# A float32 trunk layer with a two-level mixture of experts: rows scattered into one region per expert while projecting, contiguous expert steps, and the residual rows loaded a second time

## The chip, the cores and the metric

One core of one Trainium2 chip. The metric is the device time of one execution in microseconds (us), the median of several runs.

## The reference

One layer over 2080 rows of 1024 numbers (2048 of a prompt, 32 of a running stream), all in float32:

```
proj = x @ w_in ; gate_b, gate_c, val_a, val_b, gate_lru = split(proj)      # 512 columns each
u = gate_c * val_a ; y_a = gate_b * conv3(u)
xc = conv4(val_b) + bias ; y_b = rg_lru(xc) * gelu(gate_lru)                # 8 heads x 64
x = layer_norm(ALPHA * x + concat(y_a, y_b) @ w_out)
g = argmax(softmax(x @ w_router_group))                                      # 1 of 4 groups
top_v, top_i = top_k(expert logits of group g, 2)                            # 2 of its 4 experts
h = silu(x @ w1[e]) * (x @ w3[e]) * gate ; y = sum over the two experts of h @ w2[e]
x = layer_norm(ALPHA * x + y)
```

The outputs are the rows and the states (last inputs of both convolutions, last state of the recurrence), for prompt and stream. There are 16 experts with 256 hidden columns; each row goes to two of them.

## The kernel before

Every large product is made of three fp32r products: each operand is split into a high part (a copy on ACT, ScalarE) and a low part (a subtraction on DVE, VectorE), and PE (TensorE) adds high by high, high by low and low by high. The program is four blocks, one after the other; a block starts when all engines have left the one before. Inside a block the order on each engine is written out by hand, with semaphores between engines.

**Mixer and projection** (mixer and mix_project_phase, L72 to L882). The mixer goes over 4 channel groups (j), inside each over 5 chunks of 416 rows (c). A step on PE is five times 24 matmuls (L272) and six for the gates of the recurrence (L281). ACT and DVE turn the products into ya and yb, one buffer each, and SyncE stores them into y_scr (store_y, L209; stores L215, L216, L218). ACT's copy L336 of a step writes ya first and waits until the store of the step before has landed (L335); behind it on ACT stands xc_hi (L341), and on that hang DVE's xc_lo (L444) and PE's L281. Then 17 tiles of 128 rows: PE projects y (L742, 48 matmuls), DVE adds the residual row (L840), takes statistics (L845, L849), ACT normalises (L803), DVE multiplies (L863) and GpSimd adds (L701); the result x1 is stored by ACT into x1_scr (L806), and multiplied by ALPHA on ACT (L809) it is stored into acc_scr (L792). PE turns x1 (L753), ACT copies it (L788), PE makes the 20 router logits (L760), DVE copies them (L831). On PE the order of a tile t is project(t), route(t-2), turn(t-1).

**Routing** (route_phase, L934). With the logits of all 17 tiles, DVE picks groups and experts, PE counts rows (L1023, L1024), DVE works out a slot for each of the 4160 (row, expert) pairs, packed so that each expert starts on a multiple of 128, and builds one-hot tables (L1133, L1134) that PE multiplies into a table of row numbers and gates by slot (L1030). The first expert's weights are loaded and split meanwhile.

**Experts** (experts_phase, L1157). A step is 128 slots of one expert; the number of steps follows from the counts (42 here). GpSimd gathers the rows with an indirect DMA by row number (L1234); PE turns them (L1268), ACT and DVE split them (L1320, L1363), PE multiplies by w1 and w3 (L1296), ACT takes the silu (L1341), DVE multiplies by gate (L1383), PE turns that (L1303) and multiplies by w2 (L1280). The output half on ACT (L1326), half on DVE (L1369) goes to SBUF, and GpSimd adds it to acc_scr with an accumulating indirect DMA (L1246); one must have landed before the next is issued. In steps whose flag split is set the next expert's weights are split (L915, L920, L925, L929); SyncE loads weights (L1217, L1219).

**Last phase** (finish_phase, L1400). Per tile: load from acc_scr, statistics (L1453, L1456), ACT's square root and normalising pass, DVE's scale and shift (L1461, L1463), DVE's multiplication by the weight (L1459), GpSimd's addition of the bias (L1436), store.

## Time and profile before

| | us |
|---|---|
| median of 3 runs | 1322.22 |
| lowest, highest | 1317.29, 1328.05 |
| span of the profiled execution | 1314.2 |
| busy: PE, DVE, ACT, GpSimd | 1132.7, 710.5, 522.3, 298.0 |

The time of the profiled execution itself is not listed; its span, from the first to the last instruction, stands beside the three times. PEld is PE's loading of weights, which runs beside its matmuls; SPq, ACTq and POOLq are the queues of SyncE, ACT and GpSimd. A busy engine is not always the one that sets the end; the stages differ in that, and are looked at one by one.

### The profile page before, as it was taken

Reading aid. Unit: us, or ns where it says so; the run is one execution under the profiler, and the core shown is the slowest. Engines: PE = TensorE matmul, PEld = TensorE weight load, DVE = VectorE, ACT = ScalarE, POOL = GpSimd, SP = SyncE. Lnnn points to the kernel's source line nnn. Section 1 sums busy time; section 2 is a strip of 40 time slices with the busy share of each in tenths; the row PEclk is TensorE's granted clock in tenths of the full one; section 3 lists DMA queues with packets and bytes.
Section 4 is the critical chain, followed back from the end, with each engine's and each line's share of the span. In section 5 each row is a group of like instructions: output and inputs, shape, how many; then the busy total and the mean of one; then the engine's idle time right before and its main releaser. Section 6 shows DMA issues by size and latency. Waiting matters only on the chain. (4 is left out here: it accounts for less than half of the span.)

```text
span 1314.2 us, 19578 instructions
## 1 busy us (share of the span) xinstructions
PE 1132.7 (86%) x5748; PEld 1021.3 (78%) x5749; DVE 710.5 (54%) x1131; ACT 522.3 (40%) x678; POOL 298.0 (23%) x254
## 2 busy tenths in 40 slices
PE   6999999999999999999999269999999899996000
PEld 6999999999999998888887157877787778885000
DVE  5676544644555564434334755555646445531698
ACT  4554533634445453333333204444445434421222
POOL 1000000000000021121211242345535443432244
PEclk9999999999999999999999559999999999999555
DMA  5422100200120155544432535787888877764822
GB/s 181 137 85 74 56 19 19 97 19 19 35 88 13 52 166 190 173 144 160 144 128 100 205 112 179 212 279 200 267 224 233 257 194 207 206 125 62 324 112 100
DMA packets 64423, 183.95 MB, mean 140 GB/s; under 512 B 7456, under 2 KB 34096, under 8 KB 60176
## 3 DMA queue, kind: packets, MB, share of 16 engines
q1 hardware_dynamic: 42464, 104.28, 22.4%
q0 software_dynamic: 17040, 61.57, 19.1%
q10 hardware_dynamic: 4896, 17.83, 3.3%
q8 instruction: 10, 0.16, 0.1%
q14 instruction: 13, 0.11, 0.0%
HBM read 125.70 MB, written 57.96 MB: 140 GB/s over the span
## 5 line engine op out<-in xcount | busy, mean ns | idle before, releaser
L1296 PE MATMUL ps_h<-w_hi,xt_hi 128*128 x336 | 136.5, 406 | 0.0
L1296 PE MATMUL ps_h<-w_hi,xt_lo 128*128 x336 | 132.8, 395 | 0.0
L1296 PE MATMUL ps_h<-w_lo,xt_hi 128*128 x336 | 132.8, 395 | 0.0
L272 PE MATMUL ps_vb_c<-x_hi,w_hi 128*128 (+1 forms) x320 | 114.0, 356 | 10.7 <-DVE x_lo L424 10.7
L272 PE MATMUL ps_vb_c<-x_lo,w_hi 128*128 (+1 forms) x320 | 113.2, 354 | 0.0
L272 PE MATMUL ps_vb_c<-x_hi,w_lo 128*128 (+1 forms) x320 | 113.1, 353 | 0.0
L272 PE MATMUL ps_va_b<-x_hi,w_hi 128*128 (+1 forms) x320 | 112.3, 351 | 0.0
L272 PE MATMUL ps_va_b<-x_hi,w_lo 128*128 (+1 forms) x320 | 112.1, 350 | 0.0
L272 PE MATMUL ps_va_b<-x_lo,w_hi 128*128 (+1 forms) x320 | 111.9, 350 | 0.0
L1246 POOL DMA_INDIRECT acc_scr<-out_sb,id_s x42 | 76.2, 1813 | 35.4 <-POOL id_s L1242 27.9
L193 POOL DMA_DIRECT2D w_raw<-in_w_in x15 | 8.0, 531 | 328.8 <-DVE w_lo L410 320.4
L701 POOL TENSOR_TENSOR w_lo_p<-w_hi_p,w_lo_p 128x1024 f32<-128x1024 f32 x16 | 38.3, 2393 | 179.7 <-DVE w_hi_p L863 179.7
L920 DVE TENSOR_TENSOR w_lo<-w_raw,w_hi 128x2048 f32 (+1 forms) x31 | 72.4, 2335 | 11.7 <-ACT w_hi L915 11.7
L1296 PEld LDWEIGHTS ps_h<-w_hi,xt_lo 128*128 128x128 f32 x336 | 63.9, 190 | 13.8
L1296 PEld LDWEIGHTS ps_h<-w_hi,xt_hi 128*128 128x128 f32 x336 | 64.5, 192 | 12.4
L1296 PEld LDWEIGHTS ps_h<-w_lo,xt_hi 128*128 128x128 f32 x336 | 64.4, 192 | 12.5
L1268 PE MATMUL ps_x<-consts_sb,xg 128*128 128x128 f32 x336 | 47.2, 286 | 28.9 <-DMA xg<-x_scr,id_g 21.8
L272 PEld LDWEIGHTS ps_vb_c<-x_hi,w_hi 128*128 128x128 f32 x320 | 60.8, 190 | 11.6 <-issue 8.2
L1363 DVE TENSOR_TENSOR xt_lo<-ps_x,xt_hi 128x1024 fp32r<-128x1024 f32 x42 | 51.3, 1221 | 32.8 <-ACT xt_hi L1320 32.8
L1234 POOL DMA_INDIRECT xg<-x_scr,id_g x43 | 57.9, 1347 | 33.7 <-POOL id_g L1231 30.3
L1326 ACT ACTIVATE out_sb<-ps_o 128x512 f32<-128x512 f32 x42 | 25.1, 599 | 100.8 <-PE ps_o L1280 100.8
L1268 PEld LDWEIGHTS ps_x<-consts_sb,xg 128*128 128x128 f32 x336 | 38.7, 146 | 34.0 <-issue 27.1
(246 smaller groups left out, 2722.3 us busy)
## 6 DMA issues: line engine op xcount, KB each, us to landing
w_raw<-in_w SPq DMA_DIRECT2D x16, 2048.0 KB, 8.6
w_raw<-in_w SPq DMA_DIRECT2D x16, 1024.0 KB, 9.2
w_raw<-in_w_in POOLq DMA_DIRECT2D x19, 512.0 KB, 3.7
w_hi_p<-in_x_rows SPq DMA_DIRECT2D x17, 512.0 KB, 3.8
x_scr<-w_lo_p ACTq DMA_DIRECT2D x17, 512.0 KB, 2.6
acc_scr<-w_lo_p ACTq DMA_DIRECT2D x17, 512.0 KB, 2.6
v<-acc_scr SPq DMA_DIRECT2D x17, 512.0 KB, 10.5
x_raw<-in_x_t SPq DMA_DIRECT2D x20, 416.0 KB, 3.5
```

The source lines that it names most:

```text
L193: pool.dma_start(w_raw[:, i % 2], w_in[bass.ds(j * MT + i, 1)].rearrange("o p k n -> p (o k) n")).then_inc(s_wraw[i % 2], 16)
L272: mm = pe.matmul(ps[i][:, 0:CHUNK], w[:, i, k], x[:, k, bass.ds(c * CHUNK, CHUNK)], start=(k == 0 and n == 0), stop=(k == KT - 1 and n == 2))
L701: pool.tensor_tensor(x1[par], s_sb[par], ln_b, ALU.add).then_inc(s_x1, 1)
L920: eng.tensor_tensor(self.half(self.w13_lo, at, i), self.raw_half(i), self.half(self.w13_hi, at, i).bitcast(F32), ALU.subtract).then_inc(se ...
L1234: pool.indirect_dma_start(xg[:, par], None, x1_scr, bass.IndirectOffsetOnAxis(id_g[:, par:par + 1], 0)).then_inc(s_xg[par], 16)
L1246: pool.indirect_dma_start(acc_scr, bass.IndirectOffsetOnAxis(id_s[:, par:par + 1], 0), out[:, par], None, compute_op=ALU.add).then_inc(s_a ...
L1268: mm = pe.transpose(ps_x[:, k], xg[:, par, k * P:(k + 1) * P], consts[:, C_ID:C_ID + P])
L1296: mm = pe.matmul(ps_h[par][:], x[:, par, k], w[:, bass.ds(at, 1), k].rearrange("p o n -> p (o n)"), start=(k == 0 and n == 0), stop=(k == ...
L1326: act.activation(out[:, par, 0:512], ps_o[0][:], ACT.Copy).then_inc(s_oa, 1)
L1363: dve.tensor_tensor(xt_lo[:, par], ps_x[:], xt_hi[:, par].bitcast(F32), ALU.subtract).then_inc(s_xlo, 1)
```

## The change

It touches every block but leaves the products as they are.

- **Zero fills.** After channel group 0, DVE zeroes a strip of 256 columns, and SyncE issues 47 DMAs between the stores of group 0 and those of group 1: per expert, 128 rows of xs_scr and 128 entries of g_scr, then the output blocks of steps 33 to 47 of o_scr.
- **Projection.** Tiles go through a ring of eight buffers in SBUF, where they are loaded, summed and normalised in place by DVE alone (two passes, mean and weight, then 1/std and bias). The copies to x1_scr and acc_scr, ACT's two passes and GpSimd's addition are gone. PE's order is project(t) up to k = 5, turn(t-1), count matmuls, the rest of project(t), route(t-1).
- **Routing while projecting** (Router). For groups of two tiles (one of them has one) DVE assigns experts (assign) and works out places (places); each expert has a fixed region of 2080 rows in xs_scr, and a row's place is the count so far. GpSimd scatters each tile's rows twice and its gates twice with indirect DMAs (scatter). The last two groups are scattered in the experts' block, which follows at once. There, plan_steps makes the list of steps (expert, first row, split flag), the last step of an expert beginning so that it ends with its last row; slots() makes the table of output rows by token.
- **Experts.** SyncE loads 128 contiguous rows of xs_scr for PE, 128 gates, and the same 128 rows once more into another buffer. DVE evicts both halves of the output while it adds ALPHA/2 times those rows, and SyncE stores the block plainly into o_scr. Weights are loaded from GpSimd's queue. ACT evicts nothing.
- **Last phase.** GpSimd gathers the two output rows of each token; DVE adds them, takes statistics and makes both normalising passes; ACT has the square root alone.

The core of the diff:

```diff
+CAP = TOK
+ZC = 256
+XS = 4
+FEWEST = -(-TOPK * TOK // P)
+NRING = 8
+GROUPED = [(t, 2) for t in range(0, NT - 3, 2)] + [(NT - 3, 1), (NT - 2, 2)]
...
+        sp.wait_ge(s_zero, 1)
+        for e in range(NE):
+            sp.dma_start(xs_scr[e * CAP:e * CAP + P, :].rearrange("p (a d) -> p a d", d=ZC),
+                         zero.unsqueeze(1).broadcast_to((P, D // ZC, ZC))).then_inc(s_zo, 16)
+            sp.dma_start(g_scr[e * CAP:e * CAP + P, :], zero[:, 0:1]).then_inc(s_zo, 16)
+
+        for n in range(FEWEST, STEPS):
+            sp.dma_start(o_scr[n * P:n * P + P, :].rearrange("p (a d) -> p a d", d=ZC),
+                         zero.unsqueeze(1).broadcast_to((P, D // ZC, ZC))).then_inc(s_zo, 16)
         with sp.Fori(1, GROUPS - 1) as j:
...
+        dve.memset(zero, 0.0).then_inc(s_zero, 1)
...
+    def counts(self, pe, n, bank, before, ones):
+        m = GROUPED[n][1]
+        pe.wait_ge(self.s_asg, n + 1)
...
+        pe.matmul(bank[:, 0:m * NE], before, rhs, start=True, stop=True)
+        pe.matmul(bank[:, 2 * NE:(2 + m) * NE], ones, rhs, start=True, stop=True).then_inc(self.s_cnt, 1)
...
+    def scatter(self, pool, n):
+        t0, m = GROUPED[n]
+        pool.wait_ge(self.s_sl, n + 1)
+        todo = [(t, TAIL if t == NT - 1 else P, c) for t in range(t0, t0 + m) for c in range(TOPK)]
+        for t, rows, c in todo:
+            pool.indirect_dma_start(self.xs_scr, bass.IndirectOffsetOnAxis(self.sli[0:rows, t, c:c + 1], 0),
+                                    self.ring[t % NRING][0:rows], None).then_inc(self.s_sc[n % 4], 16)
+        pool.wait_ge(self.s_wts, n + 1)
+        for t, rows, c in todo:
+            pool.indirect_dma_start(self.g_scr, bass.IndirectOffsetOnAxis(self.sli[0:rows, t, c:c + 1], 0),
+                                    self.wts[0:rows, t, c:c + 1], None).then_inc(self.s_gs, 16)
...
+            early, late = list(range(KT - 2)), list(range(KT - 2, KT))
+            for t in range(NT):
+                project(t, early)
+                if t >= 1:
+                    turn(t - 1)
+                for n in ends_at(t - 2):
+                    if n == 0:
+                        pe.wait_ge(mx.s_gel, STEPS_MIX)
+                    rt.counts(pe, n, ps_c, before, ones)
+                project(t, late)
+                if t >= 1:
+                    route(t - 1)
+            turn(NT - 1)
+            route(NT - 1)
...
+                dve.scalar_tensor_tensor(out=v, in0=v, scalar=mv[:, par, 0:1], in1=ln_g,
+                                         op0=ALU.subtract, op1=ALU.mult).then_inc(s_xn, 1)
...
+                dve.scalar_tensor_tensor(out=v, in0=v, scalar=rstd[:, par:par + 1], in1=ln_b,
+                                         op0=ALU.mult, op1=ALU.add).then_inc(s_x1, 1)
+                for n in ends_at(t - 2):
+                    rt.places(dve, n, ps_c)
+                if t >= 1:
+                    logits_out(t - 1)
+                for n in ends_at(t - 1):
+                    dve.wait_ge(s_lo, t + 1)
+                    rt.assign(dve, n)
...
+            def load(s, par, h):
+                row = sp.value_load(plan[0:1, 1, bass.ds(s, 1)], min_val=0, max_val=NE * CAP - P)
+                read, there, free = (count(sp, v) for v in (s - 1, h * 32, s - (XS - 1)))
+                if not early(s, 2):
+                    sp.wait_ge(s_tx, read)
+                    sp.wait_ge(s_g[par], there)
+                sp.dma_start(xg[:, par], xs_scr[bass.ds(row, P), :]).then_inc(s_xg[par], 16)
+                if not early(s, XS):
+                    sp.wait_ge(s_ev, free)
+                sp.dma_start(gate[:, slot(par, h)], g_scr[bass.ds(row, P), :]).then_inc(s_g[par], 16)
+                sp.dma_start(flat(xr[:, slot(par, h)]), xs_scr[bass.ds(row, P), :]).then_inc(s_g[par], 16)
+
+            def store(s, par):
+                sp.wait_ge(s_ev, s + 1)
+                sp.dma_start(o_scr[bass.ds(s * P, P), :], out[:, par]).then_inc(s_st[par], 16)
+
+            def step(s, par, h, left):
+                if not early(s, 1):
+                    store(s - 1, 1 - par)
+                if left == 2:
+                    load(s + 3, 1 - par, h + 1 + par)
+
+            sp.dma_start(consts[:], consts_in).then_inc(s_con, 16)
+            sp.wait_ge(s_plan, 1)
+            for n in range(LAST - 3, LAST + 1):
+                sp.wait_ge(rt.s_sc[n % 4], rt.landed(n))
+            sp.wait_ge(rt.s_gs, 16 * TOPK * NT)
...
+            pool.dma_start(ew.w13_raw[:], w13[0]).then_inc(ew.s_r13, 16)
+            pool.dma_start(ew.w2_raw[:], w2[0]).then_inc(ew.s_r2, 16)
+            for n in (LAST - 1, LAST):
+                rt.scatter(pool, n)
...
-                act.activation(out[:, par, 0:512], ps_o[0][:], ACT.Copy).then_inc(s_oa, 1)
...
+            def evict(s, par, h):
+                dve.wait_ge(s_o, s + 1)
+                if not early(s, 2):
+                    dve.wait_ge(s_st[par], h * 16)
+                for f in range(2):
+                    c = slice(f * 512, f * 512 + 512)
+
+                    ins = dve.scalar_tensor_tensor(out=out[:, par, c], in0=flat(xr[:, slot(par, h), c]), scalar=ALPHA / 2,
+                                                   in1=ps_o[f][:], op0=ALU.mult, op1=ALU.add)
+                ins.then_inc(s_ev, 1)
...
+            rt.assign(dve, LAST)
+            rt.places(dve, LAST, ps_c)
+            dve.wait_ge(s_con, 16)
+            plan_steps()
+            ew.lo13(dve, 0, first)
+            ew.lo2(dve, 0, first)
             x_lo(0, 0)
+            slots()
...
+                for c, to in enumerate((v, v1)):
+                    pool.indirect_dma_start(to[0:n, t], None, o_scr,
+                                            bass.IndirectOffsetOnAxis(sfin[0:n, c, t:t + 1], 0)).then_inc(s_in[t], 16)
```

## Rows read from the trace of the kernel before

**Rows 1.** Stage windows: us, each engine's busy us (instructions), PE clock, DMA share, GB/s.

```profile
489.00:715.00 226.00, 225.51 (x1167) 191.74 (x1165) 94.17 (x181) 76.90 (x87) 41.50 (x21) 1.00 0.45 154
...
1207.00:1225.00 18.00, 0.07 (x1) 0.00 (x0) 0.75 (x2) 1.88 (x2) 1.75 (x2) 0.56 0.44 97
1225.00:1314.20 89.20, 0.00 (x0) 0.00 (x0) 81.41 (x102) 26.09 (x34) 39.76 (x17) 0.50 0.46 186
...
795.08:1184.52 389.44, 369.90 (x1794) 306.47 (x1795) 204.40 (x200) 164.59 (x199) 167.38 (x156) 0.99 0.76 217
```

**Rows 2.** Timeline around channel group 1's first steps: start, us, engine, line, operation.

```profile
143.35 0.43 SPq L216 DMA_DIRECT2D y_scr<-yb  x1
...
152.32 0.34 SPq L218 DMA_DIRECT2D y_scr<-ya  x1
...
166.19 0.52 ACT L336 ACTIVATE ya<-ps_vb_c 128x416 f32<-128x416 f32 x1 [2.10 <-PE ps_vb_c L272]
...
179.42 0.35 PE L281 MATMUL ps_r_i<-xc_hi,l_hi 128*128 128x420 f32 x1
```

**Rows 3.** DMA rates, 512 B pieces (window 662.7:668.5), 4 KB pieces (window 1223:1240).

```profile
GB/s 424 29 0 0 395 28 56 56 254 311 339 367 395 367 254 343 251 265 219 343 343 353 360 346 346 339 346 314 191 39 11 0 0 0 0 0 0 0 0 0
...
DMA packets 1893, 6.91 MB, mean 406 GB/s; under 512 B 207, under 2 KB 207, under 8 KB 1893
```

**Rows 4.** DMA issues: count, KB each, median us from issue to landing.

```profile
x_scr<-w_lo_p ACTq DMA_DIRECT2D x17, 512.0 KB, 2.6
...
xg<-x_scr,id_g POOLq DMA_INDIRECT x43, 7.9
...
x_hi_p<-in_w_router POOLq DMA_DIRECT2D x1, 80.0 KB, 6.7
```

**Rows 5.** Timeline of PE and DVE while projecting; the rows repeat with each tile.

```profile
619.55 1.86 PE L760 MATMUL ps_l<-x_hi_p,x_lo_p 128*128 128x20 f32 x16
...
622.09 0.70 PE L742 MATMUL ps_vb_c<-x_hi 128*128 128x512 f32 x2
...
633.17 1.86 PE L760 MATMUL ps_l<-x_hi_p,x_lo_p 128*128 128x20 f32 x16
...
646.97 1.28 DVE L840 SCALAR_TENSOR_TENSOR w_hi_p<-w_hi_p,ps_va_b 128x512 f32<-128x512 f32 x2 [6.57 <-PE ps_va_b L742]
648.29 1.29 DVE L845 BATCH_NORM_STATS2 stats<-w_hi_p 128x6 f32<-128x512 f32 x2
...
652.60 1.22 DVE L863 TENSOR_TENSOR w_hi_p<-w_hi_p 128x1024 f32<-128x1024 f32 x1 [1.18 <-ACT w_hi_p L803]
```

**Rows 6.** Timeline from the last logits to the first transpose of gathered rows.

```profile
729.88 0.18 DVE L831 COPY logits<-ps_l 128x20 f32<-128x20 f32 x1 [6.69 <-PE ps_l L760]
...
747.91 0.17 DVE L1114 TENSOR_TENSOR ecol<-ecol 128x16 f32<-128x16 f32 x1
...
775.62 1.06 POOL L1234 DMA_INDIRECT xg<-x_scr,id_g  x1 [0.62 <-POOL id_g L1228]
...
780.13 1.97 PE L1268 MATMUL ps_x<-consts_sb,xg 128*128 128x128 f32 x8 [6.58 <-DMA xg<-x_scr,id_g]
```

**Rows 7.** PE's waits in the experts: total us, times, longest us.

```profile
PE ps_x L1268 <- DMA xg<-x_scr,id_g: 21.8, 9, 6.6
```

**Rows 8.** Timeline of PE, two step starts without a stall between.

```profile
795.08 1.07 PE L1268 MATMUL ps_x<-consts_sb,xg 128*128 128x128 f32 x8 [0.32 <-issue]
...
804.41 1.04 PE L1268 MATMUL ps_x<-consts_sb,xg 128*128 128x128 f32 x8
```

**Rows 9.** The chain that ended last, in the last phase: start, us, what.

```profile
1234.98 2.33 DVE nmr L1463
...
1239.95 2.33 DVE nmr L1463
...
1304.48 2.34 POOL v L1436
...
1309.41 2.38 POOLq L1402
```

845 lines of the change are left out of this document (376 added, 469 removed).

## The prediction

> **What bounds the kernel now.** I read the stage windows first, then the timeline of each engine around each stage change, then the waits of PE, last the chain that ends the span. While projecting, PE is busy 225.5 of 226.0 us [rows 1]: PE-bound, one tile each 13.62 us (633.17 - 619.55) [rows 5]. From the last logits (729.88) to the first transpose of gathered rows (780.13) lie 50.2 us in which the whole routing runs as one chain on DVE and GpSimd [rows 6]. In the experts a step without a stall takes 9.33 us (804.41 - 795.08) [rows 8], but 39 steps take 389.4 us [rows 1], so 389.4 - 39 x 9.33 = 25.5 us are lost, 21.8 of them PE waiting for gathered rows [rows 7]. From the last expert matmul to the first statistics of the last phase are 18 us with nearly nothing on any engine, and the last phase is DVE's: 4.97 us a tile (1239.95 - 1234.98), of which 2.33 is one tiny DVE instruction that stands for as long as GpSimd's addition (2.34) runs [rows 1, 9]. The mixer is PE's; its slack matters below.
>
> The profile gives no separate time for the profiled execution; its span is 1314.2 us, 3.1 below the fastest of the three times and 8.0 below their median. I sum differences on the span and put them on the median, 1322.2.
>
> **Term 1, zero fills in the mixer: +19.** After channel group 0 the SyncE queue issues 16 + 15 fills of 512 KB from a 1 KB strip (16.25 MB in 15,872 pieces of 1 KB) and 16 fills of 128 four-byte pieces, between the stores of group 0 and those of group 1. The mixer has one ya buffer: ACT's copy L336 of step (1,1) waits until the store of ya of step (1,0) has landed. That store is issued at 152.3 and L336 runs at 166.2, while PE needs its result (through xc_hi and xc_lo) for the matmuls L281 at 179.4 [rows 2]. Now that store stands behind the fills. At 406 GB/s (4 KB pieces, a full queue) 16.25 MB take 40 us; pieces of 512 B move at some 343 GB/s in the full slices [rows 3], which gives 47. For the 2,048 four-byte pieces, 128 on each of 16 engines, the nearest row is the router weights' load of 1,024 pieces of 80 B, 6.7 us to landing [rows 4]: less some 2 us of latency, about 70 ns a piece, so 9 us. I take 41 + 9 = 50; bounds 40 (small pieces free) and 62 (343 GB/s, small pieces half as dear again). The fills start at 143.8, end at 193.8, the ya store lands 2.6 later [rows 4], then two ACT passes of 0.52 and a DVE pass of that size: PE goes on at 198.1 in place of 179.4, +19. Bounds: 40 gives +9, 62 gives +31. What is late next: ACT and DVE resume some 12 us further behind PE than in steady state, but the next matmuls each find what they need just in time; no more is added. The rings being separate is a rival.
>
> The Trainium skill (DMA: Bandwidth & Descriptors, Queues, rings and completion order) says that within one row each engine consumes descriptors in ring order, and that it takes turns between rows. If that holds, nothing that SyncE issues after the fills moves before them, and weight loads on GpSimd's row still pass: the sum above. If it does not, term 1 is 0 and the forecast falls by 19. No row of before shows the SyncE queue in such a backlog with a waiter behind it.
>
> **Term 2, projecting: +10.** PE's matmuls stay, in another order. Added: per group of tiles two small fp32 products (8 groups here), whose price the router's matmuls give: eight products in 1.86 us [rows 5], so 0.46 for two: +3.7. The projection is split at the sixth of eight k, one more change between kinds of matmul: its price lies between 0 and 0.24 (the first pair behind the transposes lasts 0.70 [rows 5], a pair goes by on average in 11.1/24 = 0.46); most of that difference is overlap, I take 0.09: 17 x 0.09 = +1.5. DVE: two adds 1.28, statistics 1.29 and 0.21, y's low part and two normalising passes at 1.22 each [rows 5] = 6.5 to x1, then in every second tile the assignment: 21 dependent small instructions at 0.17 [rows 6] plus some 0.04 of semaphore = 4.4; it ends 11.2 to 11.5 after the tile's sum starts. PE reaches the count matmuls 10.9 after (13.62 less two of eight k of a projection of 11.1 us). So about 0.5 of wait in seven groups and 2 in the last: +5 (0 to 12, the upper end at 0.26 an instruction). ACT's copy ax1, the two ACT stores a tile and GpSimd's additions go; they lay beside PE and give nothing. Scatters: 8 indirect DMAs per two tiles at 1.06 [rows 6] up to twice that, 8.5 to 17 of 27.2 us on an otherwise idle GpSimd: hidden; a ring slot is wanted again eight tiles later. Last tile: x1 comes 2.5 sooner after the last sum (no ACT pass between two DVE passes), but router and transposes of the tile before, 2.54 (622.09 - 619.55) [rows 5], that lay under that chain now lie before it: nothing. Sum +10, bounds +3 to +17.
>
> **Term 3, routing: -24.** It was 50.2. Now, from the last logits: phase change 0.4, assignment 4.5, counts on a cold PE 1.2, slots 2.0: 8.1; then GpSimd issues four row scatters and four gate scatters, 8 x 1.06 to 1.6, say 11, to 19; landing 2.6 to 3; SyncE reads its step, issues, and 512 KB land, together 4: 26. The step plan (some 30 small DVE instructions and one PE trip, done at 15), the first weights' high and low parts (done near 21) lie beside. 26 - 50.2 = -24; bounds 23 and 33, so -27 to -17. The final slot table (13 passes over 128x272) comes between the first two x_lo on DVE, beside the first expert matmuls: +0.5, in term 4.
>
> The Trainium skill (SBUF — State Buffer, SBUF: two separate sides) warns that a DMA issued from GpSimd has its descriptors written over the port that DVE locks in its two-port modes; that speaks against scatters while DVE is at work. By that rule the eight scatters would wait for DVE's passes over the first weights, as in the fourth case below.
>
> **Term 4, experts: -18.5.** Steps are counted by the same rule, so 42 stay. The loads leave GpSimd, where gather and accumulate take turns, and go to SyncE as plain loads. Per step: store, rows, rows again, 512 KB each, 3.9 us at 406 GB/s, and weights 7.8 us per expert; 42 x 3.9 + 16 x 7.8 = 289 us of some 385. The rows for step s+3 are issued after the eviction of s-1, which DVE now does alone (two passes at 0.64, half of L840's pair [rows 5]) some 1.4 after the output matmuls: 11.1 after the start of step s. They are wanted at 18.7, so they have 7.6 us; behind the store they need 2.6 + 1.3, beside a weight load twice that or a little more. I leave 6.5 of the 25.5 us of stall (15 changes of weights at 0.4): -19, and +0.5 for the first step. Bounds: 0 left, or all left, -25 to 0.5. DVE in a step with weights has 10.3 us of work for 9.33; the next step has 4, so it catches up.
>
> **Term 5, the end: 0.** After the last output: eviction 1.3, store 2.6, phase change, then gathers on GpSimd (1.06 each, 4.5 from issue to use, 780.13 - 775.62 [rows 6]; two for a tile): first DVE work at 12 in place of 18: -6. A tile costs DVE add 1.26, statistics 1.39 and 0.13, reciprocal 0.1, two passes 1.26 and 1.15: 5.3 in place of 4.97, over 17 tiles 90.0 against the 79.3 to the last multiplication: +10.7. Behind it GpSimd's 2.34 and its start go [rows 9]: -4.8. Sum 0, bounds -6 to +9.
>
> **Sum:** 19 + 10 - 24 - 18.5 + 0 = -13.5; span 1300.7, median 1308.7; I say 1308.
>
> **Rivals.** *The fills don't hold the stores* (queue served out of order, or 16 MB faster than the bounds): term 1 is 0 to 5, 1290. For it: three engines' queues work side by side today without harm; against: the fills and the stores share one, and nothing in the rows shows overtaking. Chance 0.20. *Rows come late at every step*: the load has 7.6 us, and the gathers of today have a median of 7.9 to landing [rows 4]. Beyond 7.6 each us costs 41. At 8.6, 41 us of stall replace my 6.5: +34.5, 1343, slower. It decides from a landing 0.8 later than the slack. For it: three 512 KB transfers a step share engines with 2 MB loads of longer pieces; against: a plain transfer of 512 KB lands in 2.6 where nothing runs beside it [rows 4]. Chance 0.16. *GpSimd and DVE get in each other's way*: scatters at twice the price behind DVE, routing 33 rather than 26, and the assignment at 0.26 an instruction: +7 +7, 1322, no change. Chance 0.14. The forecast has 0.50, its own range 1290 to 1326.
>
> **How the numbers follow.** About 1%, 13 us, is what a measurement here tells from no change. Of the forecast's 0.50 I give 0.27 to faster, 0.20 to same, 0.03 to slower, for 1308 lies at the border; the first rival 0.19 and 0.01 same; the second 0.15 slower, 0.01 same; the third 0.10 same, 0.04 slower. Faster 0.46, same 0.32, slower 0.22. The range 1280 to 1340 takes in the first rival whole and most of the second.
>
> **What would show it.** Right: a PE gap of about 19 us near 180 to 198 with the SyncE queue's DMA share at its full, released through ACT's L336; from last logits to first transpose near 26; PE waiting for rows under 7 us in the experts; DVE pitch 5.3 in the last phase. Wrong: no such gap, or one beyond 31; step pitch above 9.6 on average; PE waits of over 1 us at each count product; DVE instructions in the last phase stretched by GpSimd's gathers.

## The result and the profile after

| | kernel before | changed kernel |
|---|---|---|
| median of the runs, us | 1323.86 (1317.29 to 1328.05, 4 runs) | 1513.42 (1504.53 to 1518.13, 4 runs) |
| span of the profiled execution | 1314.2 | 1515.9 |
| mean granted clock of TensorE | 0.931 | 0.879 |

The ratio is 1.144, 95% interval 1.139 to 1.150. The forecast was 1308 with a range of 1280 to 1340; the result is above both.

The stage windows of the changed kernel (columns as in [rows 1]), cut at the first product of the projection, the last logits, the first transpose of expert rows and the last expert matmul:

```profile
0.00:591.00 591.00, 482.38 (x2516) 475.93 (x2518) 275.21 (x553) 227.91 (x332) 20.25 (x40) 0.92 0.44 86
591.00:857.00 266.00, 246.33 (x1260) 208.09 (x1260) 161.61 (x472) 66.71 (x82) 55.65 (x58) 0.96 0.36 119
857.00:893.00 36.00, 2.12 (x13) 1.65 (x12) 15.92 (x62) 7.12 (x5) 19.88 (x16) 0.50 0.77 262
893.00:1410.00 517.00, 429.32 (x1931) 356.20 (x1932) 243.39 (x268) 156.54 (x172) 14.87 (x28) 0.90 0.58 214
1410.00:1515.00 105.00, 0.56 (x3) 0.13 (x1) 88.54 (x122) 6.28 (x18) 35.09 (x34) 0.52 0.66 259
```

Cut at the same five places, by the starts and ends in the timelines, the stages of both kernels and the forecast for each are:

| stage (term) | before | after | measured | forecast (bounds) |
|---|---|---|---|---|
| mixer, to the first product (1) | 489.6 | 591.8 | +102.2 | +19 (9 to 31) |
| projecting, to the last logits (2) | 240.2 | 265.6 | +25.4 | +10 (3 to 17) |
| routing, to the first transpose (3) | 50.3 | 35.8 | -14.5 | -24 (-27 to -17) |
| experts (4) | 426.9 | 517.3 | +90.4 | -18.5 (-25 to 0.5) |
| last phase (5) | 107.1 | 105.4 | -1.7 | 0 (-6 to +9) |

The two largest waits of PE (us in all, times, longest). The first was 21.8 us in [rows 7], the second is new:

```profile
PE ps_x L1168 <- DMA w_lo_p<-xs_scr: 101.5, 14, 23.2
PE ps_r_i L297 <- DVE xc_lo L460: 98.4, 1, 98.4
```

**The mixer.** The timeline around the fills:

```profile
178.85 4.43 SPq L245 DMA_DIRECT2D g_scr<-x_raw  x1
...
183.91 6.57 SPq L245 DMA_DIRECT2D g_scr<-x_raw  x1
...
229.97 40.29 SPq L248 DMA_DIRECT2D o_scr<-x_raw  x15
270.90 0.73 SPq L224 DMA_DIRECT2D y_scr<-ya  x1
...
276.88 0.52 ACT L352 ACTIVATE ya<-ps_vb_c 128x416 f32<-128x416 f32 x1 [112.42 <-DMA y_scr<-ya]
...
278.53 0.72 PE L297 MATMUL ps_r_i<-xc_hi,l_hi 128*128 128x420 f32 x1 [98.42 <-DVE xc_lo L460]
```

The first four four-byte fills of g_scr (L245) hold SyncE for 0.6 us each, those from the fifth on for 4 to 8 us, which looks like a full queue. So the ya store is not even issued before the last fill has been, at 270.90. ACT's copy of ya, at 166.19 before [rows 2], now stands 112 us for its landing, and PE behind it 98 us. While the fills with four-byte pieces go out, the DMA engines are full (share above 1) and move 58 to 80 GB/s:

```profile
150.00:170.00 20.00, 20.00 (x108) 19.80 (x107) 9.06 (x20) 7.70 (x11) 0.00 (x0) 1.00 1.12 58
...
190.00:250.00 60.00, 0.00 (x0) 0.00 (x0) 0.00 (x0) 0.00 (x0) 0.00 (x0) 0.50 1.25 80
```

**The projection.** Regular turns to the transposes alternate between 13.68 and 14.6 us (13.62 in [rows 5]). The last three do not:

```profile
798.71 1.03 PE L881 MATMUL ps_r_i<-x_lo_p,w_lo_p 128*128 128x128 f32 x8
...
817.26 1.97 PE L881 MATMUL ps_r_i<-x_lo_p,w_lo_p 128*128 128x128 f32 x8 [4.72 <-DVE w_lo_p L965]
...
821.69 0.64 PE L725 MATMUL ps_g<-r_both,x_lo_p 128*128 128x32 f32 x2 [2.46 <-DVE r_both L709]
...
837.18 1.04 PE L881 MATMUL ps_r_i<-x_lo_p,w_lo_p 128*128 128x128 f32 x8
839.74 0.40 PE L725 MATMUL ps_g<-r_both,x_lo_p 128*128 128x16 f32 x2 [1.52 <-issue]
...
850.75 1.97 PE L881 MATMUL ps_r_i<-x_lo_p,w_hi_p 128*128 128x128 f32 x8 [5.80 <-DVE w_hi_p L965]
```

They take 52.0 us (850.75 - 798.71); the last three of the kernel before took 33.8 (689.34 to 723.15), with these waits:

```profile
719.54 2.27 PE L760 MATMUL ps_l<-x_hi_p,x_lo_p 128*128 128x20 f32 x16 [1.87 <-DVE logits L831]
723.15 1.97 PE L753 MATMUL ps_r_i<-x_lo_p,w_lo_p 128*128 128x128 f32 x8 [1.34 <-DVE w_lo_p L869]
```

**The routing.** From the last row scatter on:

```profile
870.41 4.47 DVE L1012 TENSOR_TENSOR w_lo<-w_raw,w_hi 128x2048 fp32r<-128x2048 f32 x2
870.61 7.32 POOL L763 DMA_INDIRECT g_scr<-r_wts,r_sli  x1 [0.30 <-issue]
...
874.81 2.27 DVE L1021 TENSOR_TENSOR w_lo<-w_raw,w_hi 128x2048 fp32r<-128x2048 f32 x1
...
881.54 0.59 POOL L1151 DMA_DIRECT2D w_raw<-in_w  x1
...
883.68 0.35 SPq L1112 DMA_DIRECT2D w_lo_p<-xs_scr  x1
...
893.23 1.12 PE L1168 MATMUL ps_x<-consts_sb,w_lo_p 128*128 128x128 f32 x4 [23.15 <-DMA w_lo_p<-xs_scr]
```

One gate scatter lasts 7.3 us, as long as DVE makes the low parts of the first weights (870.41 to 877.08) and 0.85 more, which is what such a scatter takes alone. And the first rows, issued beside 3 MB of weights, take 9.5 us to PE.

**The experts.** One step that is late:

```profile
977.29 0.53 POOL L1157 DMA_DIRECT2D w_raw<-in_w  x1 [31.30 <-DVE w_lo L1012]
978.04 0.35 SPq L1120 DMA_DIRECT2D o_scr<-w_lo_p  x1
979.40 0.34 SPq L1112 DMA_DIRECT2D w_lo_p<-xs_scr  x1
...
991.51 1.75 PE L1168 MATMUL ps_x<-consts_sb,w_lo_p 128*128 128x128 f32 x7 [6.04 <-DMA w_lo_p<-xs_scr]
```

The rows are asked for at 979.40, behind the store, and come 12.1 us later. The weights, on GpSimd's queue since 977.29, are served beside them. PE waits 6.0.

**The last phase** is as forecast; DVE's sums are 5.3 us apart, as the forecast had it:

```profile
1431.37 1.22 DVE L1434 TENSOR_TENSOR v<-v 128x1024 f32<-128x1024 f32 x1
...
1436.67 1.22 DVE L1434 TENSOR_TENSOR v<-v 128x1024 f32<-128x1024 f32 x1
```

### The profile page after: what moved, and what is told of

The parts are those of the page before. It is cut to its first block and busy times, and to the rows that moved or that the text cites. A ratio compares the mean times of both kernels' runs of the same rounds, so it can differ in the third digit from the quotient of the medians.

```text
span 1515.9 us, 20032 instructions
## 1 busy us (share of the span) xinstructions
PE 1160.7 (77%) x5718; PEld 1042.0 (69%) x5719; DVE 784.7 (52%) x1476; ACT 464.6 (31%) x608; POOL 145.7 (10%) x176
## 5 line engine op out<-in xcount | busy, mean ns | idle before, releaser
L1195 PE MATMUL ps_h<-w_hi,xt_hi 128*128 x336 | 145.2, 432 | 0.0
L1195 PE MATMUL ps_h<-w_lo,xt_hi 128*128 x336 | 139.9, 417 | 0.0
L1168 PE MATMUL ps_x<-consts_sb,w_lo_p 128*128 128x128 f32 x336 | 58.4, 331 | 105.9 <-DMA w_lo_p<-xs_scr 101.5
L1195 PE MATMUL ps_h<-w_hi,xt_lo 128*128 x336 | 138.5, 412 | 0.0
L1168 PEld LDWEIGHTS ps_x<-consts_sb,w_lo_p 128*128 128x128 f32 x336 | 48.3, 172 | 110.1 <-issue 83.8
L288 PE MATMUL ps_va_b<-x_hi,w_lo 128*128 (+1 forms) x320 | 112.7, 352 | 0.0
L297 PE MATMUL ps_r_i<-xc_hi,l_hi 128*128 128x420 f32 x40 | 14.6, 366 | 98.4 <-DVE xc_lo L460 98.4
L1228 ACT ACTIVATE xt_hi<-ps_x 128x1024 fp32r<-128x1024 f32 x42 | 43.0, 1025 | 133.2 <-PE ps_x L1168 133.2
L1277 DVE SCALAR_TENSOR_TENSOR w_lo_p<-w_hi_p,ps_o 128x512 f32<-128x512 f32 x84 | 53.9, 683 | 54.0 <-PE ps_o L1179 54.0
L297 PEld LDWEIGHTS ps_r_i<-xc_hi,l_hi 128*128 128x128 f32 x40 | 7.7, 194 | 98.9 <-DVE xc_lo L460 98.8
L460 DVE TENSOR_TENSOR xc_lo<-xc,xc_hi 128x420 fp32r<-128x420 f32 x20 | 11.9, 593 | 116.0 <-ACT xc_hi L357 116.0
```

The source lines that it names most:

```text
L288: mm = pe.matmul(ps[i][:, 0:CHUNK], w[:, i, k], x[:, k, bass.ds(c * CHUNK, CHUNK)], start=(k == 0 and n == 0), stop=(k == KT - 1 and n == 2))
L297: mm = pe.matmul(bank[:, 0:LRU_N], w[:, g], x[:], start=(n == 0), stop=(n == 2))
L1168: mm = pe.transpose(ps_x[:, k], xg[:, par, k * P:(k + 1) * P], consts[:, C_ID:C_ID + P])
L1195: mm = pe.matmul(ps_h[par][:], x[:, par, k], w[:, bass.ds(at, 1), k].rearrange("p o n -> p (o n)"), start=(k == 0 and n == 0), stop=(k == ...
L1228: act.activation(xt_hi[:, par], ps_x[:], ACT.Copy).then_inc(s_xhi, 1)
L1277: ins = dve.scalar_tensor_tensor(out=out[:, par, c], in0=flat(xr[:, slot(par, h), c]), scalar=ALPHA / 2, in1=ps_o[f][:], op0=ALU.mult, op1 ...
```

## The experiments

All start from the changed kernel. "Time" is one run beside a run of the kernel before, unless an interval is given; stages are cut in the profiled execution as above. The table holds all of them.

| kernel | time | span | mixer | project | route | experts | last |
|---|---|---|---|---|---|---|---|
| before | 1323.9 | 1314.2 | 489.6 | 240.2 | 50.3 | 426.9 | 107.1 |
| changed | 1513.4 | 1515.9 | 591.8 | 265.6 | 35.8 | 517.3 | 105.4 |
| e1_wide_fill | 1431.1 | 1429.2 | 511.1 | 264.2 | 35.4 | 512.8 | 105.7 |
| e10_apart | 1434.4 | 1432.7 | 511.9 | 263.8 | 35.9 | 515.8 | 105.4 |
| e13_adjacent | 1496.4 | 1494.6 | 570.1 | 265.6 | 35.9 | 517.4 | 105.6 |
| e14_apart64 | 1434.1 | 1432.4 | 511.8 | 264.3 | 35.8 | 514.8 | 105.8 |
| e15_apart512 | 1438.9 | 1437.2 | 512.8 | 263.9 | 35.2 | 519.7 | 105.7 |
| e6_spread_fill | 1407.9 | 1406.2 | 491.6 | 261.3 | 34.9 | 512.7 | 105.8 |
| e2_weights_sp | 1466.2 | 1464.5 | 592.5 | 265.1 | 29.6 | 471.7 | 105.5 |
| e4_copy_res | 1499.1 | 1497.4 | 586.6 | 264.3 | 35.9 | 505.1 | 105.5 |
| e5_rows_first | 1404.1 | 1402.3 | 591.9 | 265.1 | 35.9 | 403.8 | 105.6 |
| e7_rows_first_w_sp | 1419.7 | 1417.9 | 589.2 | 264.0 | 29.9 | 429.4 | 105.5 |
| e3_no_gates | 1508.3 | 1506.6 | 589.3 | 261.6 | 30.3 | 519.7 | 105.7 |
| e12_tail | 1501.1 | 1499.2 | 583.0 | 264.6 | 35.5 | 510.7 | 105.3 |
| e16_tail2 | 1503.5 | 1501.6 | 588.4 | 257.3 | 35.6 | 514.6 | 105.6 |
| e8_combo | 1303.5 | 1301.7 | 491.5 | 265.7 | 34.1 | 404.6 | 105.7 |
| e9_combo_tail | 1298.5 | 1297.1 | 490.7 | 262.9 | 26.1 | 411.6 | 105.9 |
| e11_combo_copy | 1298.1 | 1298.5 | 490.8 | 263.2 | 27.4 | 411.7 | 105.5 |
| e17_combo2 | 1295.6 | 1297.4 | 491.9 | 261.1 | 28.4 | 410.5 | 105.4 |
| e18_combo3 | 1294.6 | 1292.4 | 491.5 | 261.7 | 25.0 | 408.2 | 106.0 |

Stages that a kernel does not touch show how much they move by themselves: projecting 261.3 to 265.7, experts 510.7 to 519.7 in the kernels with late rows, and the mixer of the kernels with the fills of the changed kernel 583.0 to 592.5.

### The fills: what made them slow

**e1_wide_fill**, one piece of 512 bytes for each fill of g_scr:

```
-sp.dma_start(g_scr[e * CAP:e * CAP + P, :], zero[:, 0:1])
+sp.dma_start(g_scr[e * CAP:e * CAP + P, :].rearrange("p o -> o p"), zero[0:1, 0:P])
```

> The 16 zero fills of g_scr are each written as one piece of 512 bytes instead of 128 pieces of 4 bytes; bytes, order and queue stay. Theory A (the pairs of fills of about 5.4 us in groups 0 and 1 are nearly all the 4-byte pieces, some 4 us a fill of them, because the 15 fills of 1 KB pieces behind them went at 385 GB/s): the fills end some 64 us earlier, the wait of PE for xc_lo falls from 98 us to 25 to 40, first projection matmul at 515 to 535 in place of 591.8, time some 60 to 75 us shorter, 1440 to 1455. Theory B (1 KB pieces that fan one strip into scattered rows are slow themselves beside the stores and weight loads, the 4-byte ones are cheap): under 15 us shorter, above 1498. Everything behind the mixer unchanged.

The mixer is 80.7 us shorter, PE's wait 17.3 in place of 98.4: theory A, and by more than it asked. That is 5.0 us for each of the 16 fills. The ya store is issued at 191.06, again right behind the last fill. The same window of this kernel, beside the 58 GB/s above:

```profile
150.00:170.00 20.00, 20.00 (x107) 19.80 (x106) 9.42 (x20) 7.70 (x11) 0.00 (x0) 1.00 1.01 343
```

All traffic of the window together, nearly all of it 1 KB pieces, moves at 343 GB/s. At that rate 16.25 MB take 47 us, which the prediction had as the slow end for them.

It looked settled that a four-byte piece is dear. The next four kernels keep the wide fills and add, behind each of them, a write of 128 four-byte zeros, one from each partition, to the second 128 rows of the region, which the scatters overwrite later. They differ in the destination alone; that of e10_apart is:

```
+sp.dma_start(xs_scr[e * CAP + P:e * CAP + 2 * P, 0:1], zero[:, 0:1],
+             allow_slow_non_contiguous=True).then_inc(s_zo, 16)
```

**e10_apart**, pieces 4 KB apart:

> As the run with the gates' fills in one piece of 512 bytes, and behind each of them a further write of 128 four-byte zeros, now 4 KB apart (into column 0 of the second 128 rows of each region of xs_scr, which the scatters overwrite later). Theory A (a written piece of 4 bytes costs some 0.6 us of its DMA engine wherever it goes): the 81 us between that run and the changed kernel come back, 1500 to 1515. Theory B (the price was that neighbouring pieces of 4 bytes from 16 engines fall into the same few stretches of DRAM and wait for each other): under 15 us back, 1431 to 1446.

1434.4 against 1431.1: theory B. As many four-byte pieces as in the changed kernel cost 3 us in all, 0.8 of it in the mixer. The price is not that of a small piece.

**e13_adjacent**, **e14_apart64** and **e15_apart512**, the pieces next to each other, 64 bytes apart, 512 bytes apart:

> As the run with further four-byte zeros 4 KB apart, but the 128 pieces of each further write lie next to each other, 512 bytes in all, in the first row of the second 128 rows of the region; pieces, queue and tensor are the same as there. Theory A (neighbouring four-byte pieces written by 16 DMA engines at once wait for each other in DRAM): the 81 us come back, time 1500 to 1515, first projection matmul at 580 to 592. Theory B (what was slow in the changed kernel is something else about g_scr's fills, the tensor's place or their being wanted later): under 15 us back, 1431 to 1446.

> As the same run with the pieces 64 bytes apart (8 KB in all). Theory A (the pieces collide only when they fall into the same 64 bytes): as with 4 KB between them, 1431 to 1440. Theory B (they collide within a longer stretch, 512 bytes or more, or in one bank): well above, 1455 to 1515.

> As the same run with the pieces 512 bytes apart (64 KB in all). If 64 bytes apart is free, so is this: 1431 to 1440. If it is not, this tells whether the collision ends at 512 bytes (1431 to 1440) or lies in a longer stretch (above 1450).

Adjacent, the mixer takes 570.1 us, 59 more than with the wide fills alone, and PE waits 76.7 for xc_lo; at 64 bytes it takes 511.8 and at 512 bytes 512.8. The windows of the adjacent kernel, then of the one with 64 bytes:

```profile
150.00:170.00 20.00, 20.00 (x108) 19.80 (x107) 9.10 (x20) 7.70 (x11) 0.00 (x0) 1.00 1.15 77
```

```profile
150.00:170.00 20.00, 20.00 (x108) 19.80 (x107) 8.77 (x19) 7.70 (x11) 0.00 (x0) 1.00 0.98 308
```

Same pieces, same queue, same tensor: 77 against 308 GB/s. So theory A of the adjacent run is right in kind: four-byte pieces written next to each other hold the queue up, and 64 bytes from one to the next are enough to end it. That it is the DRAM where they wait for each other is not shown. In size it was below its range (1496.4, 1500 to 1515 expected): 3.7 us a write, not 5.0. Why a write in xs_scr costs less than one in g_scr is open, as are distances under 64 bytes.

**e6_spread_fill**, wide fills, and two of each kind behind each pair of stores of groups 1 and 2:

```
+        with sp.Fori(1, GROUPS - 1) as j:
+            with sp.Fori(0, NCH - 1) as c:
+                store_y(j, c, False)
+                for i in range(2):
+                    e = (j - 1) * 8 + c * 2 + i
...
```

> As the run with the gates' fills in one piece of 512 bytes, and the fills are no longer in one block behind channel group 0: behind each pair of stores of groups 1 and 2 stand two fills of xs_scr, two of g_scr and two of o_scr (48 fills in all, one of o_scr more than before). Theory A (the 17.3 us that PE still waited in that run come from the block of 16 MB that stands before one ya store, some 40 us long): each store now waits for at most 2 MB, 5 to 6 us, less than the slack; PE's wait for xc_lo is under 2 us, first projection matmul at 490 to 496, time 1412 to 1418, that is 95 to 101 us below the changed kernel. Theory B (what is left there is the stores' own landing beside the fills at each step): waits of 1 to 3 us in each of eight steps, time 1420 to 1432.

The wait for xc_lo is gone, the mixer takes 491.6 (489.6 before): theory A, its time (1407.9) a little under the range. What was left in e1_wide_fill, 21.5 us over the mixer of before, was the length of the block ahead of one store.

### The experts: when the rows are asked for, and beside what

**e2_weights_sp**, the loads of w13 and w2 move from GpSimd to SyncE, behind each step's rows:

```
-                pool.dma_start(ew.w13_raw[:], w13[bass.ds(e, 1)]...)
+                with sp.If(split):
+                    sp.dma_start(ew.w13_raw[:], w13[bass.ds(e, 1)]...)
...
```

> The loads of the experts' weights are issued by SyncE, each behind the row loads of the step, in the place of GpSimd; bytes and sizes stay. Theory A (the row loads land late because 3 MB of weights on another queue are served beside them, and a row of the queue that shares the DMA engines gets too little): PE's wait for the rows falls from 101 us to under 20, the experts take 430 to 450 in place of 517, time 1430 to 1450. Theory B (the sum of the bytes, 1.5 MB a step and 3 MB an expert, is what fills the engines, whoever issues it): the wait stays over 70 us, time above 1485. Theory C (the weights are now late instead, behind the store and the rows of the same queue): waits for rows are gone but PE and DVE wait for w13 by as much, time within 15 us of 1513.

Between A and C. DMA issues (count, KB, median us to landing), first of the changed kernel, then of this one:

```profile
w_lo_p<-xs_scr SPq DMA_DIRECT2D x43, 512.0 KB, 7.0
```

```profile
w_lo_p<-xs_scr SPq DMA_DIRECT2D x43, 512.0 KB, 3.8
```

With the weights off the other queue the rows land in little over half the time. But the waits only shrink:

```profile
PE ps_x L1173 <- DMA w_lo_p<-xs_scr: 40.5, 13, 16.9
PE ps_ht L1207 <- DVE hid L1299: 25.9, 8, 4.4
```

Rows now stand behind weights in one queue, and weights behind rows: PE waits for hid, DVE for ScalarE, ScalarE for w_raw. The experts take 471.7 us in place of 517.3.

The routing is 6.2 us shorter too. The weights of expert 1 are issued behind the first rows here, and these reach PE 3.3 us after their issue, where they took 9.5 in the changed kernel:

```profile
884.02 0.35 SPq L1112 DMA_DIRECT2D w_lo_p<-xs_scr  x1
...
887.32 1.97 PE L1173 MATMUL ps_x<-consts_sb,w_lo_p 128*128 128x128 f32 x8 [16.93 <-DMA w_lo_p<-xs_scr]
```

**e4_copy_res**, the residual rows copied by ScalarE, the second load left out (this undoes the third part of the change):

```
-sp.dma_start(flat(xr[:, slot(par, h)]), xs_scr[bass.ds(row, P), :]).then_inc(s_g[par], 16)
+act.activation(flat(xr[:, slot(par, h)]), xg[:, par], ACT.Copy).then_inc(s_cp, 1)
```

> The residual rows are copied by ScalarE from the transposed rows' tile, as in the kernel before, and the second load of the same 512 KB of rows is left out; all else as in the changed kernel. Theory A (order and share of the queues, not the bytes): the rows are now asked for without a load of the step before in front of them, but still stand beside the weight loads; PE's wait for rows falls from 101 us by under a third, time 1480 to 1510. Theory B (the bytes): 21.5 MB less of some 130 frees 50 us of DMA at 400 GB/s, the wait falls to under 40 us, time 1440 to 1465. ScalarE has room for a copy of 1.1 us in a step of 9.3; if it has not, its wait shows at h_hi and the time rises above 1513.

Theory A. The rows' median landing falls to 4.8, but PE still waits 90.8 us, 14 times. Experts 12 us shorter, which is little above how much that stage moves by itself.

**e5_rows_first**, the load of the rows for step s+3 ahead of the store of step s-1; gates and residual rows stay behind it:

```
                 if left == 2:
-                    load(s + 3, 1 - par, h + 1 + par)
+                    rows(s + 3, 1 - par)
+                if not early(s, 1):
+                    store(s - 1, 1 - par)
+                if left == 2:
+                    rest(s + 3, 1 - par, h + 1 + par)
```

> On SyncE the load of the rows for step s+3 is issued before the store of step s-1 instead of behind it; gates and residual rows stay behind the store; weights stay on GpSimd's queue, bytes as before. Theory A (time of asking: the rows' place is free when step s has transposed the rows of s+1, at its start, but the load stands behind a store that waits for the eviction about 11 us later, so of some 19 us only 7.6 are left): PE's wait for rows falls from 101 us to 5 to 25, the experts take 430 to 445 in place of 517, time 1430 to 1445. Theory B (bandwidth beside the weight loads: 1.5 MB a step and 3 MB an expert fill the engines): the wait only moves to gates, residual rows or weights, experts over 490, time above 1485. Theory C (a landing of 12 us beside weights is met, but hid now waits for gates or residual rows, as it did in the run with the weights on SyncE, 26 us): experts 445 to 470.

Theory A, and past its range: experts 403.8 in place of 517.3. One wait for rows is left, that for the first:

```profile
PE ps_x L1174 <- DMA w_lo_p<-xs_scr: 23.3, 1, 23.3
```

Its timeline, across a load of weights on GpSimd at 966.17:

```profile
955.58 1.04 PE L1174 MATMUL ps_x<-consts_sb,w_lo_p 128*128 128x128 f32 x8
...
960.84 0.35 SPq L1110 DMA_DIRECT2D w_lo_p<-xs_scr  x1
964.88 1.04 PE L1174 MATMUL ps_x<-consts_sb,w_lo_p 128*128 128x128 f32 x8
...
966.17 0.53 POOL L1163 DMA_DIRECT2D w_raw<-in_w  x1 [23.34 <-DVE w_lo L1012]
...
974.19 1.04 PE L1174 MATMUL ps_x<-consts_sb,w_lo_p 128*128 128x128 f32 x8
```

Steps start 9.3 us apart, weights or not. Bytes, queues and sizes are those of the changed kernel; only the moment of asking has moved (and with it the rows' landing, 5.6 us in the median in place of 7.0). In the changed kernel the rows were asked for 6.1 us before PE wanted them (979.40, wanted at 991.51 - 6.04 = 985.47). Here those issued at 960.84 fill the place that the transposes at 955.58 freed, and are wanted at 974.19, 13.3 us later.

**e7_rows_first_w_sp**, both edits together:

> Both: rows for step s+3 asked for before the store of step s-1, and the experts' weights issued by SyncE behind gates and residual rows. Theory A (asking early is enough, and the queue of the weights makes no difference once the rows have 18 us): time within 8 us of the run with the rows first alone. Theory B (the weight loads on another queue still hold the rows back by more than their slack): this run is over 15 us shorter than that one. Theory C (in one queue the rows now stand behind the 3 MB of weights of the step before, and the gates behind them): over 10 us longer than that one.

Theory C: 15.6 us longer than e5_rows_first, experts 429.4. Once rows are early, the weights are better left on their own queue.

### The gates and the routing

**e3_no_gates**, the scatters of L763 and the wait for them left out, gates read from a fixed place:

> The gates are not scattered, and each step reads its gates from the first 128 (zero) entries of g_scr, so the experts' part of the output is left out. Theory A (scatters of 128 four-byte pieces cost about 4 us of DMA each, and hold up both the y load of tile 16 in the projection's tail and the first row load of the experts): projecting takes 10 to 15 us less than 265.9, and from the last logits to the first transpose of rows are 26 to 29 in place of 35.6; time 1490 to 1500. Theory B (the tail of the projection is the order of work on DVE and the memset, the routing gap is the weight loads on GpSimd's queue): the projection stays within 4 us of 265.9, the gap within 3 us of 35.6, time 1508 to 1517.

By the time, theory B, but the routing falls by 5.5 us, more than it allowed and less than theory A asked. Projecting falls by 4.0, which is within its own movement. So the gate scatters are nothing in the projection, and more than half of the 9.8 us by which the routing missed its forecast.

**e12_tail**, y's low part of tile 16 on DVE behind the normalising passes of tile 14:

```
-                if t + 2 < NT:
+                if t + 3 < NT:
...
+                if t + 3 == NT:
+                    dve.wait_ge(s_yhi, t + 3)
+                    dve.tensor_tensor(y_lo[par], y_raw[par], y_hi[par].bitcast(F32), ALU.subtract).then_inc(s_ylo, 1)
```

> The changed kernel with one edit: y's low part of tile 16 is made on DVE after the normalising passes of tile 14, not before them. Theory A (the two long turns at the end of the projection come from this order: the pad's memset, the late load of tile 16 and y's low part stand before x1 of tile 14): PE's waits of 4.8 and 2.5 us go, the projection takes 258 to 261 in place of 265.6, time 5 to 7 us shorter. Theory B (the wait moves to tile 16's own product, since its y's low part now comes after two passes of 1.2 us): under 2 us.

The projection is 1.0 shorter; the wait only changed hands. ScalarE and DVE in that kernel:

```profile
803.20 1.06 ACT L915 ACTIVATE x_hi<-x_hi_p 128x1024 fp32r<-128x1024 f32 x1 [11.39 <-DMA x_hi_p<-y_scr]
```

```profile
804.47 0.17 DVE L962 RECIPROCAL rstd<-std 128x1 f32<-128x1 f32 x1 [5.92 <-ACT std L917]
```

DVE now waits 5.9 us for ScalarE's standard deviation of tile 14, which stands behind y's high part of tile 16, which waits for its load. (Most of the 17 us less in the span lies in the mixer and the experts, which the edit does not touch.)

**e16_tail2**, ScalarE's high part of tile 16 put behind it as well:

> The changed kernel with y's low part of tile 16 on DVE, and now y's high part of tile 16 on ScalarE too, behind the normalisation of tile 14. Theory A (the long turn comes through ScalarE: its standard deviation of tile 14 stands behind the high part of tile 16, which waits for a load that lands 5.6 us after the pad's memset; DVE then waited 5.9 us for it): PE's wait for x1 of tile 14 (4.7 in the changed kernel, 2.6 with DVE's order alone) is gone, the wait for the assignment behind it falls from 4.4 to under 2.5, the projection takes 258 to 261. Theory B (the load then is late for tile 16's product instead): PE waits for y's low part at its start, projection above 263.

The projection takes 257.3 in place of 265.6, and no wait for x1 of tile 14 is left: theory A, the cause of that wait is the order on ScalarE. The last three turns take 47.2 us in place of 52.0, so 4.9 of the 8.3 us are the edit's; the others lie at the start of the projection, where it changes nothing (first wait of the turns 0.65 in place of 2.58, second turn 13.75 in place of 15.30). What theory A said of the wait for the assignment missed, for it grew:

```profile
PE ps_g L725 <- DVE r_both L709: 8.6, 8, 5.6
```

### All together

**e8_combo**, spread and wide fills, rows first, the first two row loads ahead of the wait for the gate scatters:

> Spread fills with the gates' fills in one piece, rows asked for before the store, and the first two row loads no longer wait for the gate scatters. If the mixer's stall (98 us), the experts' waits for rows (some 75 us of the 90 too many) and some 5 us of the routing gap are independent costs, the time is 1513 - 98 - 75 - 5 = 1335, range 1325 to 1350, a little above or level with the kernel before (1322). If the waits in the experts depend on the clock or on bandwidth rather than on when the rows are asked for, 1400 or more.

1303.5, 32 less than the sum of waits had it and below its range; the experts came down by 112.7 us where 75 had been counted, because each stall took its clock with it (below).

**e9_combo_tail** adds DVE's order of e12_tail, expert 1's weights behind `pool.wait_ge(s_tx, 1)`, and the last two groups' gate scatters behind all their row scatters. **e11_combo_copy** is that with ScalarE's copy in place of the second load. **e17_combo2** is e9_combo_tail with ScalarE's order too, **e18_combo3** that without the wait before the weights.

> The combination that ran in 1303.5 us (fills spread, the gates' fills in one piece, rows asked for before the store, first rows ahead of the wait for gates) and three edits more: in the projection, y's low part of tile 16 is made after the normalising passes of tile 14, not before them; expert 1's weights wait until step 0 has transposed its rows; the last two groups scatter all their rows before any gate. Theory A: the tail gives 4 to 7 us (PE waits 4.8 for x1 of tile 14 there and 2.5 for the assignment behind it), the routing 4 to 7 (first rows land beside no 3 MB of weights: 9 us from issue become 4): 1289 to 1296, and below the kernel before by 2%. Theory B (the projection's length varies by 4 us from run to run for other reasons and the rows' landing is set by the scatters, not by the weights): within 4 us of 1303.

> As the combination with the three edits, and the residual rows are copied by ScalarE again, the second load of the rows left out. Theory A (once rows are asked for early, DMA is no limit and ScalarE has room): same time within 4 us, so that this part of the change is worth nothing by itself. Theory B (the 21.5 MB less make landings shorter where rows, store and weights meet): 4 to 10 us shorter. Theory C (the copy of 1.1 us stands on ScalarE between the high parts of x and of the weights, which some steps wait for): 5 to 20 us longer.

> The combination with three edits (1298.5 us) and ScalarE's order of the run beside this one. If the tail's stall is ScalarE's order, 3 to 5 us less: 1293 to 1296, below the kernel before by 2%. If not, within 2 us of 1298.

> As the run beside it, but expert 1's weights no longer wait for the first transposes. Theory A (that wait only moved the stall: the routing came down by 8 us, but the first change of weights then made hid wait 6 us, experts 411.6 in place of 404.6): routing 30 to 34, experts 404 to 406, the time within 3 us of the run beside it. Theory B (the rows' early landing is worth more): this run is 4 to 8 us longer.

| kernel | median of 4 runs | ratio to before, 95% interval |
|---|---|---|
| e9_combo_tail | 1298.49 | 0.983 (0.979 to 0.987) |
| e11_combo_copy | 1298.10 | 0.982 (0.979 to 0.985) |
| e17_combo2 | 1295.64 | 0.979 (0.975 to 0.982) |
| e18_combo3 | 1294.55 | 0.980 (0.976 to 0.985) |

All four are faster than the kernel before, by about 2%; the intervals leave open whether it is more or less than that. e9_combo_tail fell between its two theories, and e17_combo2 is 2.9 us below it, with runs that overlap. Between e9 and e11 there is nothing: with rows asked for early, the second load and ScalarE's copy cost the same. Between e17 and e18 there is nothing either: the wait before the weights did no good, and what shortened the routing was the order of the scatters. e18_combo3 from its last row scatter on:

```profile
765.25 0.85 POOL L757 DMA_INDIRECT xs_scr<-w_hi_p,r_sli  x1 [0.30 <-issue]
766.40 7.33 POOL L768 DMA_INDIRECT g_scr<-r_wts,r_sli  x1 [0.30 <-issue]
773.39 1.46 SPq L1122 DMA_DIRECT2D w_lo_p<-xs_scr  x2
...
778.22 1.11 PE L1191 MATMUL ps_x<-consts_sb,w_lo_p 128*128 128x128 f32 x4 [12.33 <-DMA w_lo_p<-xs_scr]
```

The gate scatter that lasts as long as DVE's passes is still there, but the rows no longer wait for it, and they reach PE 4.8 us after their issue in place of 9.5: routing 25.0.

## Why the prediction was wrong

**Term 1, +19, measured +102.** The mechanism was right: the ya store behind the fills, ACT's copy, xc_lo, PE's matmul. The chosen rate for 1 KB pieces was optimistic, the bound right (343 GB/s). The step that failed is "about 70 ns a piece, so 9 us" for the four-byte fills: they took 81. The row it rested on, the router weights' 80-byte pieces [rows 4], was a load, and the price belongs to writes that fall next to each other. Its upper bound, "half as dear again", had no row under it either, for none of the rows was a small write (and 47 with 13.5 for them makes 60.5, not the 62 given). With those fills free, the kernel (e1_wide_fill) came at +21.5, where the prediction's own steps with 47 us for the fills give some 16.

**The rule on ring order** (the Trainium skill, DMA: Bandwidth & Descriptors, Queues, rings and completion order) was taken as holding. The trace agrees as far as it can tell: the ya store, once issued, landed 6.0 us later (270.90 to 276.88; 1.9 in the median of such stores), so it stood some 4 us in the ring. The rest of ACT's 112 us it had not been issued, because SyncE itself stood in its fills from 144.20 to 270.26. The order of the program on SyncE, not that in the ring, was nearly the whole wait.

**Term 2, +10, measured +25.** The regular turns came as forecast: 13.68 and 14.6 in place of 13.62, that is +0.5 a turn, and PE's waits before the count products came to 5.4 us, as forecast. What failed is "last tile: nothing". The last three turns cost 18 us more than before. PE stood 14.5 us in them (4.7 for x1 of tile 14, 2.5 and 1.5 before two count products, 5.8 for x1 of tile 16), where it had stood 3.2; that is 11 of the 18. Another 2.8 are the last quarter of tile 14's projection, which the split moved behind the first of these turns, and some 4 are the count products and matmuls at the lower clock behind the waits. e16_tail2 gives 5 back, by an order on ScalarE that the prediction did not look at.

**Term 3, -24, measured -14.5.** Two steps failed. The eight scatters, "say 11, to 19", ended 24.1 us after the last logits, because one gate scatter waited 6.4 us for DVE. And "SyncE issues, and 512 KB land, together 4" put the weights of expert 1 nowhere: the first rows took 9.5 beside them, 3.3 where they were issued behind the rows (e2_weights_sp). The landing between, 2.1, held. With gates last and rows not waiting for them (e18_combo3) the routing took 25.0, one less than the 26 forecast.

**The rule on the shared port** (the Trainium skill, SBUF — State Buffer, SBUF: two separate sides) says that GpSimd can't write the descriptors of its DMAs while DVE runs in a two-port mode. The prediction took that for DVE's passes over the weights, but these are two-input subtractions (TENSOR_TENSOR in the rows), of which the same section (under Who interferes with whom) says that they have no two-port mode, contend only with GpSimd's reads and, as it infers, leave the descriptors alone. A scatter is held all the same: the one issued at 870.61 ends 0.85 us after DVE's last pass over the weights, in the changed kernel as in e9_combo_tail and e18_combo3 (7.32, 7.33, 7.33 us). In e17_combo2 three scatters take 3.04, 1.89 and 1.90, and each ends some 0.84 after another one of the three passes. What of a scatter waits, and why it gets in between two passes in one kernel and not in another, is not shown. The hold did not catch all eight scatters, as the prediction had it for that rule, but one of them: 6.4 us, near the 7 of the rival in which GpSimd and DVE are in each other's way. That rival had this part right in its size.

**Term 4, -18.5, measured +90.** The slack of 7.6 us was nearly right (6.1): behind the store the rows are asked for that late. The failed step is the landing "beside a weight load twice that or a little more" of 3.9: it was 12.1 us. The second rival had the mechanism, but as a delay at each of 41 steps; it came at 13 steps, by some 6 us. Of the 101.5 us of waiting, 23.2 belong to the first rows, in the routing; 78.3 lie in the experts, where the kernel before had 15.2 (21.8 less the 6.6 of its own first rows, [rows 6]). That is 63 of the 90. The rest is the clock. The matmuls of the experts keep PE busy for 429.3 us in the changed kernel at a granted clock of 0.90, for 401.9 in the kernel before at 0.98, 27 less, and for 395.3 in e18_combo3, where rows never come late (windows from first transpose to last matmul, before and e18_combo3):

```profile
780.00:1207.00 427.00, 401.92 (x1932) 332.25 (x1932) 215.28 (x212) 177.16 (x213) 174.65 (x164) 0.98 0.72 204
...
778.00:1186.00 408.00, 395.33 (x1931) 331.08 (x1932) 241.75 (x268) 156.59 (x172) 17.61 (x32) 0.98 0.77 277
```

So, against e18_combo3, 78 us of waiting cost 34 more at the lower clock (1.2 in place of 2.4 GHz for a while after each wait: eight transposes take 1.97 us behind a wait, 1.03 otherwise). With the rows asked for early (e5_rows_first) the experts take 403.8, within 5 us of what the forecast gave (426.9 - 18.5 = 408.4).

On weights beside rows, what e2_weights_sp shows (7.0 us to landing beside the other queue, 3.8 without) agrees with the Trainium skill (DMA: Bandwidth & Descriptors, Queues, rings and completion order): each DMA engine takes turns between the rows of queues that have work, a packet at a time. The prediction cited this page for order within a queue and did not draw the price for the neighbour from it.

**Term 5, 0, measured -1.7**, by its steps: 5.3 us a tile.

**The whole.** The sum failed by two terms, each a transfer priced from a row of another kind. Three things made the changed kernel slow: four-byte fills next to each other, a block of fills ahead of one store, and rows asked for behind a store. With these mended (e8_combo) one run took 1303.5 beside 1317.6 of the kernel before; with the scatters and the tail of the projection in another order as well, the same idea is about 2% faster. The range was too narrow by its own account: it ended at 1340, and the second rival stood at 1343.

## What to carry to other kernels

Ask for a load when its place comes free, not behind a store that waits for something later; a queue is a list of waits, and each issue inherits those before it. Never write neighbouring four-byte pieces from many partitions at once: turn the strip into one piece, or put 64 bytes between them. Where the trace has no row for a kind of transfer, take that term's upper end from a test or leave it wide, and add the clock to what short waits of PE cost: here 13 waits of 6 us brought 34 us more on top of 78.
